# A two-block kernel's first recurrence: queries' norm taken together with the output's norm, from sums packed four heads to a matmul group

## The reference

```
def rms_norm(x, w):
    y = xf * lax.rsqrt(jnp.mean(xf * xf, axis=-1, keepdims=True) + EPS)
def l2_norm(x):
    return xf * lax.rsqrt(jnp.sum(xf * xf, axis=-1, keepdims=True) + EPS)
...
q_a = l2_norm(qkv[..., :DN_QK].reshape(B, S, DN_HEADS, DN_DK))
k_a = l2_norm(qkv[..., DN_QK:2 * DN_QK].reshape(B, S, DN_HEADS, DN_DK))
...
o_a = gated_delta_rule(q_a, k_a, v_a, g_a, beta_a)
o_a = rms_norm(o_a, dn_norm_w[l]) * jax.nn.silu(dn_z.reshape(B, S, DN_HEADS, DN_DV))
```

## Time and profile before

| | |
|---|---|
| median of 3 runs | 1988.59 us (1987.72 to 1990.28) |
| the profiled execution's own time | 1986.86 us |
| its span, first to last instruction | 1985.1 us |
| PE busy | 1929.6 us, 97% of the span |
| POOL busy | 966.4 us, 49% |
| DVE busy | 903.7 us, 46% |
| ACT busy | 810.8 us, 41% |
| mean granted clock of PE | 0.991 |

### The profile page before, as it was taken

The page is one execution under the profiler, slowest core; times in us unless marked ns, Lnnn a source line. Parts: engine busy times, 40 slices in busy tenths (PEclk is TensorE's granted clock), DMA queues, the critical chain, the costliest instruction groups (busy, mean ns, idle before and its releaser), DMA issues.

```text
span 1985.1 us, 26416 instructions
## 1 busy us (share of the span) xinstructions
PE 1929.6 (97%) x10306; PEld 1567.3 (79%) x10306; DVE 903.7 (46%) x1473; ACT 810.8 (41%) x1067; POOL 966.4 (49%) x742
## 2 busy tenths in 40 slices
PE   6999999989999999999999999999999999999997
PEld 3787888867788878888888678878877888888886
DVE  2678659964431333222102885369945521112101
ACT  4568342365552333232223763243337543232221
POOL 3637335643144545655665580033542556554662
PEclk9999999999999999999999998999999999999999
DMA  7312045431112322222234320034221322323222
GB/s 292 107 64 81 27 175 212 174 108 43 44 66 105 137 79 103 99 93 106 85 107 138 127 64 23 12 112 111 102 85 44 128 100 92 106 85 106 105 90 82
DMA packets 30827, 199.40 MB, mean 100 GB/s; under 512 B 5488, under 2 KB 7664, under 8 KB 9712
## 3 DMA queue, kind: packets, MB, share of 16 engines
q1 hardware_dynamic: 30704, 197.72, 28.1%
HBM read 188.79 MB, written 4.19 MB: 97 GB/s over the span
## 4 chain that ended last, share of the span: by engine, by line
PE 85%; DVE 6%; ACT 4%; POOL 3%; DMA 1%; issue 1%; SPq 0%; DVEq 0%; POOLq 0%; ACTq 0%
PE ps L465 23%; PE ps L467 22%; PE ps L466 22%; PE ps L541 2%; POOL WL L2748 1%; PE ps L483 1%; PE ps L484 1%; PE ps L947 1%; PE ps L934 1%; PE ps L571 1%; PE ps L506 1%; DVE ar L2090 1%; ACT WH L1435 1%; PE ps L681 1%; DMA ar<-ada_dram 1%
## 5 line engine op out<-in xcount | busy, mean ns | idle before, releaser
L2748 POOL TENSOR_TENSOR WL<-raw,WH 128x512 fp32r<-128x512 f32 x588 | 784.6, 1334 | 862.2 <-ACT WH L1435 819.7
L465 PE MATMUL ps<-hH,WH 128*128 128x512 f32 x1560 | 618.6, 397 | 8.6 <-ACT ar L1728 5.5
L467 PE MATMUL ps<-hH,WL 128*128 128x512 f32 x1560 | 608.4, 390 | 0.0
L466 PE MATMUL ps<-arR,WH 128*128 128x512 f32 x1352 | 526.0, 389 | 0.0
L1435 ACT CAST WH<-raw 128x2048 fp32r<-128x2048 f32 x147 | 280.9, 1911 | 465.8 <-DMA raw<-panels_dram 464.4
L465 PEld LDWEIGHTS ps<-hH,WH 128*128 128x128 f32 x1560 | 293.3, 188 | 82.1 <-issue 11.4
L467 PEld LDWEIGHTS ps<-hH,WL 128*128 128x128 f32 x1560 | 293.2, 188 | 62.3
L466 PE MATMUL ps<-xL,WH 128*128 128x512 f32 x792 | 309.5, 391 | 0.0
L466 PEld LDWEIGHTS ps<-arR,WH 128*128 128x128 f32 x1352 | 253.8, 188 | 53.1 <-issue 0.5
L465 PE MATMUL ps<-arR,WH 128*128 128x512 f32 x584 | 228.0, 390 | 0.0
L467 PE MATMUL ps<-arR,WL 128*128 128x512 f32 x584 | 227.2, 389 | 0.0
(11 more groups left out here) (395 smaller groups left out, 2266.2 us busy)
## 6 DMA issues: line engine op xcount, KB each, us to landing
raw<-panels_dram SPq DMA_DIRECT2D x145, 1024.0 KB, 4.9
ar<-ada_dram SPq DMA_DIRECT2D x12, 2048.0 KB, 11.1
xT<-xT_dram SPq DMA_DIRECT2D x2, 2048.0 KB, 8.7
out_dram<-xT SPq DMA_DIRECT2D x8, 512.0 KB, 2.8
ar<-ar SPq DMA_DIRECT2D x12, 256.0 KB, 7.4
xT<-out_dram SPq DMA_DIRECT2D x1, 2048.0 KB, 10.8
wide<-wide_dram SPq DMA_DIRECT2D x1, 1024.0 KB, 4.9
ar<-ar SPq DMA_DIRECT2D x8, 128.0 KB, 3.7
```

The lines of the kernel that those rows point to most:

```text
L465: mm(out, lhs[0], rhs[0], start=first, stop=False)
L466: mm(out, lhs[0], rhs[1], start=False, stop=False)
L467: return mm(out, lhs[1], rhs[0], start=False, stop=final)
L2748: ins = tt(WL[:, n % SLOTS, c], raw[:, n % SLOTS, c], WH[:, n % SLOTS, c].bitcast(F32), ALU.subtract)
```

## The change

Four things are changed, all in the first block.

The queries are no longer normalised. Their eight sums are now made by `query_sums`: four matmuls with weights 32 columns wide, each into its own 32 partitions of one bank, for heads 0 to 3 and, added on top into other rows, for heads 4 to 7. DVE turns that bank into the tile EXTRA (a factor of EPS for each token and head). The first group stands behind the projection of job 17 and the second behind job 19, where before four sums each stood behind jobs 16 and 17. Squares 12 to 15 reuse the four buffers once the whole first group has read them; before, each waited for the one sum that had read its buffer.

The output's sums of squares are made in the same form (`output_sums`), DVE adds EXTRA, ACT makes two tiles of 1/rms for four heads each, and `output_spread` brings each head's row back to all partitions with a matmul of weights of 32 rows by 128 columns into a bank of its own. DVE multiplies the output straight from those banks.

The z projections are interleaved with these groups and have banks named by hand; the common turn of banks is advanced by four so that later work has the banks it had. The low part of the panel for z jobs 4 and 5 is due at the end of the second output sums rather than of the eighth.

The constant table has three more matrices of 128x128.

```
-DUE_AT = {("z", 1): (("p5", 2, 1), 0), ("z", 2): ("onorm", 7), ("ai", 1): ("gmean", 0)}
+DUE_AT = {("z", 1): (("p5", 2, 1), 0), ("z", 2): ("onorm", 1), ("ai", 1): ("gmean", 0)}
...
+            def four_sums(out, sel, tiles, squared, n0, start=True, stop=True):
+                for q in range(HALF):
+                    pe.wait_ge(squared, n0 + q + 1)
+                    ins = mm(out[32 * q:32 * q + 32, :], sel, tile(tiles[q]), start=start, stop=stop)
+                return ins
+            def spread(name, g, src, sel, banks=ALL_BANKS):
+                for q in range(HALF):
+                    b = slice(32 * q, 32 * q + 32)
+                    begin(name, HALF * g + q, banks)
+                    end(mm(pst(name, HALF * g + q), const(sel)[b, :], src[b, :], start=True, stop=True))
...
                 project("qkv", h_mix, 1, i0=16, banks=(0,))
-                unit_sums(2)
                 project("qkv", h_mix, 1, i0=17, banks=(3,))
-                unit_sums(3)
+                query_sums(0)
                 project("qkv", h_mix, 1, i0=18, banks=(0,))
                 project("qkv", h_mix, 1, i0=19, banks=(3,))
+                query_sums(1)
...
                 project("z", h_mix, 1, banks=(3,))
-                for h in range(H):
-                    column_sums("onorm", h, [tile(24 + h % 4)], [(sem("onorm_sq"), h + 1)], banks=(6, 7, 0, 2, 1, 4, 5))
-                project("z", h_mix, 4, i0=1)
+                output_sums(0)
+                project("z", h_mix, 1, i0=1, banks=(0,))
+                output_sums(1)
+                output_spread(0)
+                project("z", h_mix, 1, i0=2, banks=(6,))
+                output_spread(1)
+                project("z", h_mix, 1, i0=3, banks=(3,))
+                project("z", h_mix, 1, i0=4, banks=(0,))
+                if counting:
+                    jobs.turns[ALL_BANKS] += 4
                 ada(4)
...
-                unit_rstds(2)
...
-                unit_rstds(3)
...
                 for g in range(2):
-                    rstds("onorm", range(4 * g, 4 * g + 4), (28, 29, 30, 31), 1.0 / P, sem("o_rstd"), sem("o_scaled"))
+                    emptied(act, "onorm", g)
+                    link(af(tile(28 + g), tile(28 + g), ACT.Ln, scale=1.0 / P))
+                    link(af(tile(28 + g), tile(28 + g), ACT.Exp, scale=-0.5), sem("o_rstd"), g + 1)
...
-                steps(units, 9)
+                steps(units, 7)
+                filled(dve, "l2_query")
+                link(ts(tile(EXTRA), pst("l2_query"), EPS, EPS * P * P, ALU.add, ALU.mult), *read("l2_query"))
+                steps(units, 2)
...
+                for g in range(2):
+                    filled(dve, "onorm", g)
+                    link(tt(tile(28 + g), pst("onorm", g), tile(EXTRA), ALU.add), *read("onorm", g))
                 for h in range(H):
-                    dve.wait_ge(sem("o_rstd"), h + 1)
-                    link(stt(tile(V0 + h), tile(V0 + h), col("dn_norm"), tile(28 + h % 4), ALU.mult, ALU.mult), sem("o_scaled"), h + 1)
+                    filled(dve, "onorm_unit", h)
+                    link(stt(tile(V0 + h), tile(V0 + h), col("dn_norm"), pst("onorm_unit", h), ALU.mult, ALU.mult), *read("onorm_unit", h))
...
                     if n >= 4:
-                        pool.wait_ge(pe_done, last["l2", n - 4])
+                        pool.wait_ge(pe_done, last["l2", n - 4] if n < 12 else last["l2_query", 0, 0])
...
-                ahead(pool, "l2", 11)
-                for n in range(8, 16):
-                    if n == 12:
-                        ahead(pool, "qkv", QKV_ORDER[18])
-                    pool.wait_ge(sem("l2_rstd"), n + 1)
-                    x = tile(Q0 + QKV_ORDER[n])
-                    link(tt(x, x, tile(28 + n % 4), ALU.mult), sem("qk_normed"), n + 1)
+                ahead(pool, "qkv", QKV_ORDER[17])
+                ahead(pool, "qkv", QKV_ORDER[18])
+                pool.wait_ge(sem("qk_normed"), 8)
```

More of the change, by code:

```diff
@@ L93 @@
 CONST_128 = ["ident", "ones", "top64", "low64", "same64", "head_sums", "utri", "neg_after", "strict64",
-             "incl64"]
+             "incl64", "half_sums", "first_of32", "middle_of32"]
 def constants():
@@ L111, in constants @@
     m["incl64"] = same & (j <= c)
+    m["half_sums"] = (c >= 16) & (c < 32)
+    m["first_of32"] = j % 32 == 0
+    m["middle_of32"] = j % 32 == 16
     sq = np.stack([np.asarray(m[k], np.float32) for k in CONST_128], 1)
@@ L141 @@
 ALL_BANKS, CHAIN_BANKS, DENSE_BANKS = tuple(range(8)), tuple(range(6)), (6, 7)
-STEP_BANKS, OUT_BANKS, SUM_BANKS = (0, 1, 2, 3), (4, 5), (1, 2, 4, 5)
+STEP_BANKS, OUT_BANKS = (0, 1, 2, 3), (4, 5)
 RM_BANKS = ((1, 2), (3, 4), (7, 0), (1, 2))
@@ L543, in column_sums, with half_sums @@
                 end(ins)
+            def half_sums(second):
+                return const("half_sums")[:, 0:32] if second else const("half_sums")[:, 16:48]
+            def four_sums(out, sel, tiles, squared, n0, start=True, stop=True):
[8 more added lines that the diff above has]
+                    end(mm(pst(name, HALF * g + q), const(sel)[b, :], src[b, :], start=True, stop=True))
             def halves(qt):
@@ L673, in unit_sums, with query_sums, output_sums, output_spread @@
                     for n in range(4 * g, 4 * g + 4):
-                        column_sums("l2", n, [tile(24 + n % 4)], [(sem("l2_sq"), n + 1)], banks=ALL_BANKS if g < 2 else SUM_BANKS)
+                        column_sums("l2", n, [tile(24 + n % 4)], [(sem("l2_sq"), n + 1)])
+                def query_sums(g):
+                    if g == 0:
+                        begin("l2_query", 0, (2,))
+                    end(four_sums(pst("l2_query"), half_sums(g), (24, 25, 26, 27), sem("l2_sq"), H + HALF * g, start=(g == 0), stop=(g == 1)),
+                        ("l2_query", 0), g)
+                def output_sums(g):
+                    begin("onorm", g, (6, 7))
+                    end(four_sums(pst("onorm", g), half_sums(g), (24, 25, 26, 27), sem("onorm_sq"), HALF * g))
+                def output_spread(g):
+                    pe.wait_ge(sem("o_rstd"), g + 1)
+                    spread("onorm_unit", g, tile(28 + g), "middle_of32" if g else "first_of32", banks=(1, 2, 4, 5))
                 def head_products(what, t, hf, banks):
@@ L801, in block_1 @@
                 dense(8)
-                pe.wait_ge(sem("qk_normed"), 16)
+                pe.wait_ge(sem("conv_silu"), 16)
                 for t in range(NT):
@@ L1584, in unit_rstds @@
                     logarithm_next()
-                    rstds("l2", range(4 * g, 4 * g + 4), (28, 29, 30, 31), 1.0, sem("l2_rstd"), sem("qk_normed"),
-                          power_bias=(col("qscale") if g >= 2 else 0.0))
+                    rstds("l2", range(4 * g, 4 * g + 4), (28, 29, 30, 31), 1.0, sem("l2_rstd"), sem("qk_normed"))
                 for n in range(8):
@@ L1646, in block_1 @@
                 conv_tap(19)
-                act.wait_ge(sem("qk_normed"), 16)
+                act.wait_ge(sem("qk_normed"), 8)
                 act.wait_ge(sem("unit_rows"), 2)
@@ L1692, in block_1 @@
                     filled(act, "mq", i)
-                    if i == 0:
-                        act.wait_ge(sem("o_scaled"), 8)
                     if i == 8:
@@ L2832, in block_1 @@
                     if h >= 4:
-                        filled(pool, "onorm", h - 4)
+                        filled(pool, "onorm", 0)
                     link(tt(tile(24 + h % 4), tile(V0 + h), tile(V0 + h), ALU.mult), sem("onorm_sq"), h + 1)
```

## The result

| | before | changed |
|---|---|---|
| median (5 runs each) | 1988.59 us (1986.48 to 1990.28) | 1997.82 us (1995.74 to 1998.97) |
| profiled execution, its span | 1986.86, 1985.1 | 1995.82, 1994.0 |
| PE busy | 1929.6 us | 1926.8 us |

What follows compares the result with a forecast made beforehand. PE, busy 97% of the span, was taken to bound the kernel. +4.3 us at the query sums and -2.4 at the output's norm gave +1.9 on 1988.59, so 1990.5 us, range 1985.5 to 1994.0.

Steps and rivals of the forecast that it cites:

- Price of the groups: New sums and spreads on PE: 1.05 us per group of four; PE's work falls from 13.7 to 6.3 us.
- that rival: Output spreads run one after the other at 3.6 us a group, giving 1993.6 us; chance 0.12.
- The stall before job 18: At the query sums, PE stands still 7.9 us for POOL's low part of the panel; job 18 starts at 175.1.
- Its cold clock: Lower clock behind the wait before job 18: booked at 2.1 us, bounds 0 and 4.2.
- Place one: Query sums up to the join L757: late by 4.3 us in all.
- Behind the join: After L757, the 2.7 us wait before the recurrence stays and all moves by 4.3 us.
- Place two: Output's norm up to ada(4): gain of 2.4 us, PE waiting 1.9 us for DVE; bounds -4.5 and +0.7.
- The step that failed: After ada(4), PE sets the pace until the wait before 444.93, so the difference is carried to the end.
- the sum of 1.9: Whole kernel: +4.3 at place one and -2.4 at place two make +1.9 us.
- a further give-back: At ada(5) to ada(8), badly falling splits under DVE lose up to 2 us more, 1992.5 us; chance 0.16.
- the signs that I had named for being wrong: Job 18 starting without a wait, a spread over 3 us, or a new wait over 2 us after ada(4).

Runs made afterwards that it cites:

- the filled wait: Changed kernel with 28 further matmuls on PE filling the wait before job 18: 1991.36 us, ratio 1.0016.
- changed twice: The changed kernel and its unaltered repeat beside the other kernels: 1997.82 us the first time; again 1997.04 us, ratio 1.0040.
- panel first: Changed kernel with SyncE loading the z job's next column panel ahead of adaLN weights 7 to 11: 1996.29 us, ratio 1.0032.
- query half: Changed kernel with the eight old output sums, leaving out the queries' share of the output's EPS term: 1997.79 us, ratio 1.0038.
- output half: Kernel before with only the new output sums and spreads, queries normed as before: 1992.92 us, ratio 1.0022.
- split first: Changed kernel with GpSimd splitting job 18's panel ahead of squares 12 and 13: 1993.05 us, ratio 1.0019.
- two and four edits: Two edits: changed kernel with split first and panel first together, 1989.07 us, ratio 0.9998; four edits has its own line.
- four edits: Changed kernel with split first, panel first, products 4 before output multiplications 4 to 7, z jobs 3 and 4 exchanging banks: 1987.23 us, ratio 0.9990.
- those with fills: The kernels of four edits and one fill (1981.96 and 1982.42 us) and of four edits with two fills (1984.84 us).
- four edits and one fill: Four edits plus 9 further matmuls in the wait at 218 us: 1981.96 us, ratio 0.9955; measured again 1982.42 us, 0.9973.
- before with one fill: Kernel before with 9 further matmuls in its own wait at 216 to 218.7 us: 1990.27 us, ratio 1.0011.
- two fills: Four edits and one fill plus 11 further matmuls in the wait before job 19: 1984.84 us, ratio 0.9978.

## Why the prediction was wrong

Point by point, by its own steps.

*Price of the groups.* Right: 1.07 us for sums of four against 1.05, and 1.14 for a spread against 1.05. The spreads run side by side, and that rival is out. The 3.07 times of the Trainium skill ("TensorE: Matmul & The Clock Gate", section "Measured speedup vs the span model") gave 1.12; the trace agrees.

*The stall before job 18.* Right in cause and size: 7.78 us behind POOL's split against 7.9, job 18 at 174.85 against 175.1. Its cold clock was mis-sized: booked at 2.1 us, 1.3 by the filled wait. Place one came to +3.5 at the join against +4.3.

*Behind the join.* The step said that the 2.7 us wait before the recurrence stays and all moves by the same amount. The wait stayed at 2.71 us, but a wait of the same length that kept the clock before lost it now: 16 records took 3.65 us instead of 2.05. That is hardly chance alone. The clock was low there in all five profiles of kernels in which job 18 starts late (changed twice, panel first, wait filled, query half), and full in all five of unfilled kernels in which it does not (before, output half, split first, two and four edits). I booked 0; it was 1.7. Why a late job 18 should do this some 45 us further on is not shown: with the wait filled the clock was full behind job 18 and low here all the same.

*Place two.* -1.75 at ada(4) against -2.4, in the main as booked (PE waited 2.04 us against 1.9): VectorE's products(4) ended 28.4 us behind the first output sum in both kernels (307.78 and 302.56), since a split of 6.75 us still lay under them and the last multiplications came half a microsecond later than reckoned, and ScalarE's SiLU of z job 4, in the bank that ada(4) asks for, ended at the same time.

*The step that failed* is "What follows is paced by PE until the wait before 444.93 ..., so the difference is carried to the end". It cost 5.0 of the 6.5 us by which the sum of 1.9 fell short of 8.4. I had named a further give-back of up to 2 us between ada(5) and ada(8), "if splits under DVE fall badly", and had counted VectorE's slack against PE, but not what VectorE's products let go: SP's queue, in which a panel stands behind the adaLN load. A delay of VectorE became a delay of a transfer, of a cast, of SiLUs and of VectorE's next products, and these, begun late, lay beside GpSimd's splits for most of their time and took 12.1 us instead of 8.3. The splits beside VectorE were thus rightly feared, and their price put too low: +3.3 us at ada(7), a new wait of 3.09 us, and +1.7 at ada(8) by the low clock behind it. A new wait of over 2 us behind ada(4) was also one of the signs that I had named for being wrong. Moving that one load away removed the wait.

*The size of the whole.* Of the +8.4 us, low clock behind waits is 1.3 + 1.7 + 1.7 = 4.7, and the other 3.7 are waits that the shorter groups don't pay for. The forecast had 2.1 us of clock. The clock's share looks larger over all runs: mean span times mean granted clock is 1967.3 us for before (15 runs) and 1966.8 for the changed kernel (5 runs, the second time); the remainder, span times what the clock lacked, is 19.9 and 28.7. Waiting at the low clock is in that remainder too (about half of the wait before job 18), so it doesn't part waits from cold work. The same product is 1960.7 us for the four edits and 1961.4 to 1962.7 for those with fills: by it the edits are worth 5 to 7 us, and what is seen of them in a median hangs on the clock.

The kernel that beats both most clearly is the one with four edits and one fill: 1982.42 us, ratio 0.9973 (0.9963 to 0.9983).

Open: what in an execution decides whether the clock falls behind a wait of 2 to 3 us, and whether the second recurrence runs cold; why the filled waits moved the medians by more, and in one kernel by less, than their places; and which of the last two of the four edits (products sooner, banks exchanged) matters, since they ran only together.

## What to carry to other kernels

When work is taken off an engine, follow every queue that it then reaches sooner or later, the transfer queue above all: a load that waits for a buffer holds up whatever stands behind it. Then look again at what GpSimd does beside VectorE. Put a price on the clock behind every wait of 2 us or more, old ones too, as something that can come or not. And before you put several instructions behind one common wait, look at what stands behind them on their engine: POOL's two squares cost little, the split behind them cost the gain.

## What the runs showed of the hardware

- Waits of 2.0 to 3.1 us of PE were followed by the full clock in some executions of nearly the same program and by half of it in others (at ada(4): 2.04 us and the full clock in the changed kernel, 2.02 us and 0.57 over 8 us with the panel first).
- A wait of 3.3 us near 727 us is in every one of these kernels. The clock stayed full behind it in six profiles (before, before with one fill, the changed kernel twice, split first, output half) and fell in the other eight, among them all five with two or four edits, which reached it 2 to 4 us sooner. That gave back about 1.8 us of what the edits had gained by the gate. The kernel before, and then the four edits:

```profile
724.00:738.00 14.00, 10.74 (x41) 1.00 0.20 75
```

```profile
724.00:738.00 14.00, 10.74 (x34) 0.76 0.18 71
```

- In the second recurrence the clock fell without a wait over 1.2 us ahead of it: PE was busy 3.90 of 6.00 us at 1204 to 1210 in the kernel before, and then had 0.51 for 17 us. PE in this kernel:

```profile
1204.00:1210.00 6.00, 3.90 (x86) 1.00 0.01 3
1210.00:1227.00 17.00, 17.00 (x274) 0.51 0.01 2
```

- Whether it does decides about 8 us, more than the whole change was forecast to do: between two casts of ScalarE around this stretch lie 101.1 us with the four edits (1184.4 to 1285.5) and 93.0 with two fills (1182.3 to 1275.3), where the clock stayed full.
- A split on GpSimd slows VectorE's multiplication of two SBUF tiles, and not the same multiplication with its second tile in PSUM: before, four took 6.06 us beside a split (and 3.32 almost alone); in the changed kernel four from PSUM took 3.10 us, both from 288.28, mostly beside the split of 285.11 to 290.50, and from 295.04, beside none. Before, and then the changed kernel:

```profile
286.82 6.06 DVE L2344 SCALAR_TENSOR_TENSOR ar<-ar,cols 128x512 f32<-128x512 f32 x4 [4.15 <-ACT ar L1502]
```

```profile
288.28 3.10 DVE L2392 SCALAR_TENSOR_TENSOR ar<-ar,cols,ps 128x512 f32<-128x512 f32 x4 [0.33 <-PE ps L564]
```
